# Banded attention scores: two products a block, with high and low queries in the two halves of the partitions

## What is computed

```
def swa_sink_attention(q, k, v, sinks):
    ...
    qc = q.reshape(b, nc, CHUNK, A_KV_HEADS, grp, d)
    kb = window_chunks(k.reshape(b, nc, CHUNK, A_KV_HEADS, d), A_WINDOW_CHUNKS)
    ...
    sc = jnp.einsum('bnqkgd,bnjkd->bnkgqj', qc, kb).astype(jnp.float32) * (d ** -0.5)
    ...
    p = e / (jnp.sum(e, -1, keepdims=True) + jnp.exp(sink - m))
    o = jnp.einsum('bnkgqj,bnjkd->bnqkgd', p.astype(v.dtype), vb)
```

## Time and profile before

| | us |
|---|---|
| median of 3 runs | 2661.86 (2660.55 to 2664.36) |
| profiled execution | 2663.14 |
| its span, first to last instruction | 2661.4 |
| its mean granted TensorE clock | 0.969 |
| PE busy | 2491.0 |
| DVE busy | 1658.8 |
| ACT busy | 1217.2 |
| POOL busy | 452.3 |
| end of the first stage's last product | 545 |

### The profile page before, as it was taken

One profiled execution on the slowest core, in us unless ns is written; L12 is line 12 of the kernel. 1 busy time (PEld: TensorE's weight loads), 2 busy tenths in 40 slices (PEclk: granted clock), 3 DMA queues, 4 the chain that ended last, 5 costly groups with the idle time before them and its releaser, 6 DMA issues. The chain is left out here.

```text
span 2661.4 us, 42306 instructions
## 1 busy us (share of the span) xinstructions
PE 2491.0 (94%) x12879; PEld 2092.6 (79%) x12880; DVE 1658.8 (62%) x3322; ACT 1217.2 (46%) x2075; POOL 452.3 (17%) x526
## 2 busy tenths in 40 slices
PE   5999999979999999998999999499999999999990
PEld 4888888868888888887788887388888888888880
DVE  5655455567677776766644455775785557657856
ACT  4333232244454544545111112375785557657856
POOL 0111111110110111100223331111211121112110
PEclk9999999989999999999999999599999999999995
DMA  6333333566756757535544434487897789769957
GB/s 199 122 106 102 102 102 102 153 182 194 213 182 194 216 172 205 196 132 214 177 136 139 142 111 166 171 293 278 284 382 245 226 296 327 242 225 324 381 158 260
DMA packets 233100, 535.86 MB, mean 201 GB/s; under 512 B 42945, under 2 KB 93377, under 8 KB 230961
## 3 DMA queue, kind: packets, MB, share of 16 engines
q1 hardware_dynamic: 164560, 422.55, 45.9%
q0 software_dynamic: 16416, 56.57, 8.8%
q10 hardware_dynamic: 52032, 55.61, 6.0%
HBM read 415.63 MB, written 119.01 MB: 201 GB/s over the span
## 5 line engine op out<-in xcount | busy, mean ns | idle before, releaser
L2543 DVE TENSOR_TENSOR e_wl<-rw_raw,e_wh 128x1024 fp32r<-128x1024 f32 (+1 forms) x384 | 446.6, 1218 | 24.7 <-ACT e_wh L2456 24.6
L2456 ACT ACTIVATE e_wh<-rw_raw 128x1024 fp32r<-128x1024 f32 (+1 forms) x384 | 376.9, 1049 | 6.5 <-PEq L74 6.5
L1228 PE MATMUL b_pg<-b_g_wh,jb_w_low 128*128 128x512 f32 x1024 | 336.6, 402 | 1.4 <-DVE b_g_out L1437 1.1
L2406 PE MATMUL e_p_gu<-e_wh,e_xh 128*128 128x512 f32 (+1 forms) x784 | 310.8, 396 | 0.8 <-DVE e_xl L2548 0.8
L2408 PE MATMUL e_p_gu<-e_wl,e_xh 128*128 128x512 f32 (+1 forms) x784 | 306.4, 391 | 0.0
L2407 PE MATMUL e_p_gu<-e_wh,e_xl 128*128 128x512 f32 (+1 forms) x784 | 305.9, 390 | 0.0
L1228 PEld LDWEIGHTS b_pg<-b_g_wh,jb_w_low 128*128 128x128 f32 x1024 | 185.1, 189 | 36.1 <-issue 3.8
L1286 ACT ACTIVATE b_th<-b_t 128x512 fp32r<-128x512 f32 (+3 forms) x160 | 85.3, 533 | 263.4 <-PE b_t L1210 255.2
L1228 PE MATMUL b_pg<-b_g_wl,jb_w_low 128*128 128x512 f32 x512 | 204.5, 400 | 0.0
L1377 DVE TENSOR_SCALAR_CACHE_REDUCE b_sc<-b_s 128x512 f32<-128x512 f32 (+4 forms) x320 | 175.8, 580 | 34.8 <-PE b_s L1199 32.7
L386 PE MATMUL j_pg<-qkv_w_hi,j_xh 128*128 128x512 f32 (+1 forms) x512 | 192.4, 376 | 2.4 <-DVE qkv_w_lo L682 2.4
(11 more groups left out here) (414 smaller groups left out, 5529.3 us busy)
## 6 DMA issues: line engine op xcount, KB each, us to landing
rw_raw<-w_gate_up SPq DMA_DIRECT2D x256, 512.0 KB, 6.3
rw_raw<-w_down SPq DMA_DIRECT2D x128, 512.0 KB
jb_w_low<-xt_hi SPq DMA_DIRECT2D x64, 512.0 KB, 3.8
jb_w_low<-xt_lo SPq DMA_DIRECT2D x64, 512.0 KB, 4.8
gates<-b_g_out ACTq DMA_DIRECT2D x64, 256.0 KB, 5.8
m_gt<-gates SPq DMA_DIRECT2D x16, 1024.0 KB, 8.3
jb_lead<-qk_hi SPq DMA_DIRECT2D x36, 256.0 KB, 7.1
jb_lead<-qk_lo SPq DMA_DIRECT2D x36, 256.0 KB, 7.8
```

Source lines behind the costliest of these rows:

```text
L1228: last = nc.tensor.matmul(pg[:], x_side, w_side, start=(q == 0), stop=(q == PASSES - 1))
L2406: nc.tensor.matmul(p_gu[p][:], xh[:, at], hi, start=(k == 0), stop=False)
L2456: nc.scalar.activation(wh[:, slot(e, s), :], raw[:, s:s + 1, :], ACT.Copy).then_inc(w_hi, 1)
L2543: nc.vector.tensor_tensor(wl[:, slot(e, s), :], raw[:, s:s + 1, :], f(wh[:, slot(e, s), :]), ALU.subtract).then_inc(w_lo, 1)
```

## The change

A group's queries get a tile of their own over all 128 partitions: `qa[:, g]` has the high queries of g in the 64 rows of g and their low queries in the other 64. `ks[:, g]` has the high keys of g in both halves. The low keys of both groups stand in a new tile `kl`, each in its own rows. One product of `qa[:, g]` with `ks[:, g]` over 128 rows then gives high by high plus low by high, and a second one over the 64 rows of g gives high by low. A block is made of two products in place of three, a unit of 8 in place of 12.

To fill these places, ACT's high copy is made for each group apart (64 partitions each), DVE's low part too, DVE copies the high keys to the other half, and ACT keeps the old low keys with an instruction of its own. To make room for `kl`, `by_sin` moves into the tile `lg`, where the lambdas were loaded; these are loaded later, after the last rotation, behind the store of the last tile's pieces.

```
@@ __init__ of Chunk0, project_phase
-        by_sin = ph.sb("by_sin", [P, BANK])
+        by_sin = chunk0.by_sin
...
-        qa = ph.sb("qa", [P, 2, A_Q], F32R)
-        ks = ph.sb("ks", [P, 2, 3 * CHUNK], F32R)
+        qa = ph.sb("qa", [P, A_KV, A_Q], F32R)
+        ks = ph.sb("ks", [P, A_KV, 3 * CHUNK], F32R)
+        kl = ph.sb("kl", [P, 3 * CHUNK], F32R)
...
+        def rows_of(g):
+            return slice(g * HD, (g + 1) * HD)
+
+        def banded_of(r, g, rows):
+            if r == 0:
+                return qa[rows, g, :].rearrange("p (c i n) -> p c i n", c=2, n=CHUNK)
+            return ks[rows, g, 0:P]
@@ load_chunk0 and the end of SP's work
-                for n, lam in enumerate(lambdas):
-                    sp.dma_start(chunk0.lam[:, n, :], lam.to_broadcast([P, HD])).then_inc(chunk0.lam_in, 16)
...
             store_rows(sp, STAGED0[2], STAGED0[3], slice(SEQ - P, SEQ), last_stored)
+            sp.wait_ge(rotated, 4 * NT + 2)
+            for n, lam in enumerate(lambdas):
+                sp.dma_start(chunk0.lam[:, n, :], lam.to_broadcast([P, HD])).then_inc(chunk0.lam_in, 16)
             sp.wait_ge(v_lo_done, 2 * (NT - 1) + 4)
@@ scores_of
+                def seen(keys, b):
+                    return keys[:, 0:P] if b >= 2 else keys.rearrange("p (n c) -> p n c", c=CHUNK)[:, 0:3:2, :]
...
+                        k_hi, k_lo = seen(ks[:, g, :], b), seen(kl[rows, :], b)
...
-                    nc.tensor.matmul(out, qh[:, bs], k_hi, start=True, stop=False)
-                    nc.tensor.matmul(out, qh[:, bs], k_lo, start=False, stop=False)
-                    last = nc.tensor.matmul(out, ql[:, bs], k_hi, start=False, stop=True)
+                    nc.tensor.matmul(out, qa[:, g, bs], k_hi, start=True, stop=False)
+                    last = nc.tensor.matmul(out, qa[rows, g, bs], k_lo, start=False, stop=True)
@@ pieces, on ACT
-                            nc.scalar.activation(ks[:, :, P:P + CHUNK], f(ks[:, :, CHUNK:P]), ACT.Copy).then_inc(k_kept, 1)
+                            nc.scalar.activation(ks[:, :, P:P + CHUNK], f(ks[:, :, CHUNK:P]), ACT.Copy)
+                            nc.scalar.activation(kl[:, P:P + CHUNK], f(kl[:, CHUNK:P]), ACT.Copy).then_inc(k_kept, 1)
...
+                    if r < 2:
+                        for g in range(A_KV):
+                            own_rows = rows_of(g)
+                            done = nc.scalar.activation(banded_of(r, g, own_rows), turned_of(r, last)[own_rows], ACT.Copy)
+                        done.then_inc(qk_hi_done, 1)
@@ low, on DVE
+                    if r < 2:
+                        for g in range(A_KV):
+                            own_rows, others = rows_of(g), rows_of(1 - g)
+                            if r == 0:
+                                low_part = banded_of(r, g, others)
+                            else:
+                                nc.vector.tensor_copy(banded_of(r, g, others), f(banded_of(r, g, own_rows)))
+                                low_part = kl[own_rows, 0:P]
+                            done = nc.vector.tensor_tensor(low_part, turned_of(r, last)[own_rows], f(banded_of(r, g, own_rows)), ALU.subtract)
+                        done.then_inc(qk_lo_done, 1)
```

More of the change, by code:

```diff
@@ L99, with __init__ @@
 class Chunk0:
-    def __init__(self, ph, lam):
+    def __init__(self, ph, lam, by_sin):
         self.w = ph.sb("w0", [P, KD, BANK], F32R)
@@ L109, in __init__ @@
         self.raw = self.rows[:].rearrange("p u (a n) -> p (u a) n", n=BANK)
-        self.lam = lam
+        self.lam, self.by_sin = lam, by_sin
         self.qk_in, self.v_in, self.lam_in = ph.sem("qk_in"), ph.sem("v_in"), ph.sem("lam_in")
@@ L413, in scores_of @@
                     after(pe, o_added, 2 * t + g - 1)
-                rows = slice(g * HD, (g + 1) * HD)
-                qh, ql = (qa[rows, half, :] for half in range(2))
+                rows = rows_of(g)
+                def seen(keys, b):
+                    return keys[:, 0:P] if b >= 2 else keys.rearrange("p (n c) -> p n c", c=CHUNK)[:, 0:3:2, :]
                 for b in range(NB):
                     out = blocks(unit_bank(g, last_tile))[:, b, :]
[L418 to L421, removed]
+                    if isinstance(t, int) and t == 0 and b < 2:
+                        k_hi, k_lo = ks[:, g, 0:CHUNK], kl[rows, 0:CHUNK]
                         out = out[:, 0:CHUNK]
                     else:
-                        k_hi, k_lo = (ks[rows, half, :].rearrange("p (n c) -> p n c", c=CHUNK)[:, 0:3:2, :] for half in range(2))
-                        out = out.rearrange("p (n c) -> p n c", c=CHUNK)
+                        k_hi, k_lo = seen(ks[:, g, :], b), seen(kl[rows, :], b)
+                        if b < 2:
+                            out = out.rearrange("p (n c) -> p n c", c=CHUNK)
                     bs = slice(b * P, (b + 1) * P)
-                    nc.tensor.matmul(out, qh[:, bs], k_hi, start=True, stop=False)
-                    nc.tensor.matmul(out, qh[:, bs], k_lo, start=False, stop=False)
-                    last = nc.tensor.matmul(out, ql[:, bs], k_hi, start=False, stop=True)
+                    nc.tensor.matmul(out, qa[:, g, bs], k_hi, start=True, stop=False)
+                    last = nc.tensor.matmul(out, qa[rows, g, bs], k_lo, start=False, stop=True)
                 last.then_inc(scores, 1)
@@ L581, in pieces @@
                             act.wait_ge(qk_lo_done, 4 * t)
-                            nc.scalar.activation(ks[:, :, P:P + CHUNK], f(ks[:, :, CHUNK:P]), ACT.Copy).then_inc(k_kept, 1)
+                            nc.scalar.activation(ks[:, :, P:P + CHUNK], f(ks[:, :, CHUNK:P]), ACT.Copy)
+                            nc.scalar.activation(kl[:, P:P + CHUNK], f(kl[:, CHUNK:P]), ACT.Copy).then_inc(k_kept, 1)
                             act.wait_ge(k_kept, t)
-                    nc.scalar.activation(staged_of(0, r), turned_of(r, last), ACT.Copy).then_inc(qk_hi_done, 1)
+                    if r < 2:
[4 more added lines that the diff above has]
+                    else:
+                        nc.scalar.activation(staged_of(0, r), turned_of(r, last), ACT.Copy).then_inc(qk_hi_done, 1)
                 def v_part(j):
@@ L810, in low @@
                     dve.wait_ge(qk_hi_done, 4 * t + r + 1)
-                    nc.vector.tensor_tensor(staged_of(1, r), turned_of(r, last), f(staged_of(0, r)), ALU.subtract).then_inc(qk_lo_done, 1)
+                    if r < 2:
[3 more added lines that the diff above has]
+                                low_part = banded_of(r, g, others)
+                            else:
+                                nc.vector.tensor_copy(banded_of(r, g, others), f(banded_of(r, g, own_rows)))
+                                low_part = kl[own_rows, 0:P]
+                            done = nc.vector.tensor_tensor(low_part, turned_of(r, last)[own_rows], f(banded_of(r, g, own_rows)), ALU.subtract)
+                        done.then_inc(qk_lo_done, 1)
+                    else:
+                        nc.vector.tensor_tensor(staged_of(1, r), turned_of(r, last), f(staged_of(0, r)), ALU.subtract).then_inc(qk_lo_done, 1)
                 if first:
@@ L2633, in program @@
         with Phase(nc, "jb") as both:
-            chunk0 = Chunk0(both, lg[:].rearrange("p t n -> p (t n)")[:, 0:4 * HD].rearrange("p (n d) -> p n d", d=HD))
+            logits = lg[:].rearrange("p t n -> p (t n)")
+            chunk0 = Chunk0(both, logits[:, 0:4 * HD].rearrange("p (n d) -> p n d", d=HD), logits[:, 0:BANK])
             with Phase(nc, "qkv") as ph:
```

## The result

| | before | after |
|---|---|---|
| median | 2662.43 (4 runs, 2660.55 to 2664.36) | 2712.53 (4 runs, 2711.34 to 2714.29) |
| profiled execution | 2663.14 | 2712.85 |
| its span | 2661.4 | 2711.1 |
| its mean granted clock | 0.969 | 0.959 |
| end of the first stage's last product | 544.9 | 595.5 |

The ratio is 1.019, 95% interval 1.018 to 1.021: slower, as forecast, but by 50 us and not by 26. The forecast was 2688 with a range up to 2704, so the direction was right and the size about half.

A forecast was written before the change was run, and what follows sets the result against it. PE sets the pace in the first stage's loop. Switches +23.8 us, waits for low queries +2.2 and lambda loads 0 give +26.0 on 2663.1, 2689.1; the median is 1.3 lower, so 2688 us, range 2683 to 2704.

The forecast's parts named there:

- What bounds the kernel: First stage's loop: PE is busy all the time and sets the pace; a tile costs the sum of PE's steps.
- The price of a switch: Score products on PE: each change between 64-row and 128-row form costs 0.15 us; +23.8 us in sum.
- The split copies: ACT's and DVE's query and key work: nothing in the loop, 1.1 us each in tiles 0 and 15, +2.2 us.
- The lambda loads: SP's queue, four loads moved behind the last pieces' store: v store about a microsecond later, hidden, 0 us.
- The clock: PE's granted clock in the loop's score stretch: the sum left it at 1.00, adding nothing.
- rival 2: Loop's score stretch: the clock also falls, 6 falls of 1.6 us, 2688 + 10 = 2698 us; chance 25%.
- The upper bound that stands in the same paragraph: Clock falls in the score stretch: at most 1.7 us each, in 15 pairs at most 25 us.
- Rival 1: Score products: switches are free within an accumulation, loads 0.11 us apart, 12.4 us faster, 2650 us; chance 8%.

The follow-up runs named there:

- the first experiment: The changed kernel with the three 64-row products of before, keeping the new layout, split and extra copies and moved lambda loads: 2666.07 us, 1.0020 of the kernel before.
- experiment 8: Changed kernel with zero-padded low keys (128 rows), first unit's probability turn behind group 2's first step, DVE starting after g = 0's copy: 2651.52 us, 0.9961.
- Experiment 2: Changed kernel with each group's low keys padded with zeros, so the second product also goes over 128 rows, no switches: 2658.27 us, 0.9986 of before.
- experiment 3: Changed kernel with a unit's four high products first and its four low ones after, 4 switches a pair: 2662.50 us, ratio 1.0005 to the kernel before.
- experiment 6: Changed kernel with the previous tile's g = 1 score unit moved behind group 1, 16 switches in two stretches: 2690.09 us, ratio 1.0109 to before.
- experiment 7: Changed kernel with zero-padded low keys (128 rows, no switches) and each product cut into two of 64 key columns: 2690.72 us, 1.0115 of before.
- experiment 4: Changed kernel with blocks ordered high, low, low, high, 8 evenly spread switches a pair: 2677.51 us, ratio 1.0059 to the kernel before.
- experiment 5: Changed kernel with high and low forms alternating only in the g = 0 unit, g = 1 zero-padded, 8 packed switches: 2672.57 us, 1.0042 of before.

## Why the prediction was right and wrong

**What bounds the kernel: right.** PE is busy for nearly all of the loop in every kernel here, and everything behind the stage moved rigidly.

**The price of a switch: right, 0.145 us against 0.15.** Two switches at the edges of a pair were a fair sample for sixteen inside it. A pair takes 4.43 us against 4.50 forecast, since the loads are 0.255 and not 0.26 us apart. The single units: 2.39 and 2.16 against 2.43 and 2.19. The second one's loads, to be held against the earlier trace rows:

```profile
582.63 0.19 PEld L440 LDWEIGHTS j_pg<-j_ks,j_qa 128*128 128x128 f32 x1
582.89 0.18 PEld L441 LDWEIGHTS j_pg<-j_kl,j_qa 64*128 64x128 f32 x1
...
584.43 0.18 PEld L441 LDWEIGHTS j_pg<-j_kl,j_qa 64*128 64x128 f32 x1
584.68 0.42 PEld L413 LDWEIGHTS j_pt<-ident,j_by_cos 128*128 128x128 f32 x4
```

The Trainium skill, "TensorEngine Tiling (Array Packing)", Key Properties, has the same rule, that a change of the tiling mode drains TensorE; the runs agree and put 0.145 us on it, for 128-column products.

**The split copies: right in kind.** Nothing in the loop from the third pair on, as the first experiment shows. In tile 15 the copies and subtractions come one after the other, each as long as one over all rows, and PE's wait is 2.37 us, 1.3 more than in the earlier trace rows and not 1.1:

```profile
563.08 1.19 ACT L600 ACTIVATE j_qa<-j_pt 64x512 fp32r<-64x512 f32 x2 [0.16 <-PE j_pt L413]
564.31 1.39 DVE L838 TENSOR_TENSOR j_qa<-j_pt,j_qa 64x512 fp32r<-64x512 f32 x2 [0.55 <-ACT j_qa L600]
565.85 0.44 PE L413 MATMUL j_pt<-ident,j_by_cos 128*128 128x128 f32 x1 [2.37 <-DVE j_qa L838]
```

DVE's 0.55 us of waiting end only when ACT has both halves, which is what experiment 8 mends. A part of this step's price I had not seen: behind waits of 2.4 us in the last tile the clock fell once for 3.4 us in five of the kernels (the changed one and those of experiments 2, 3, 6 and 7), but behind the same wait not in those of experiments 1, 4 and 5.

**The lambda loads: right.** The loads are off the path at their new place, which answers to the earlier trace rows; the v stores follow at 592.64, and the last outputs wait for PE as before, 1.4 us behind its last product. The four loads hold the queue for 2.2 us there and not for the 4.8 that the sum carried over from their old place, which changes nothing:

```profile
588.88 0.54 SPq L347 DMA_DIRECT2D lg<-lambda_q  x1
...
592.64 0.34 SPq L349 DMA_DIRECT2D v_hi<-j_staged  x1
...
596.97 2.51 SPq L281 DMA_DIRECT2D oa<-jb_rows  x4
```

**The clock: wrong, and this is the step that failed.** The sum put the clock at nothing; in the changed kernel it took some 27 us of the stage (24.7 up to the last pair, 2.7 from it on). The forecast's own sum, with the clock left up, is a good forecast of experiment 6, where the clock does stay up in the loop (2688 against 2690.1). The changed kernel is rival 2, which I gave 25% and sized at "6 falls of 1.6". There were 15, one at each pair, of 1.45 us each, and three of them twice as long. The upper bound that stands in the same paragraph, 25 us, would have given 2688 + 25 = 2713, and 2712.5 was measured. That this fits so closely is partly luck: it counts 15 falls of at most 1.7 us, while three of the falls were twice as long and a sixteenth came in the last tile, and the switches took 22.7 us and not 23.8. What misled me was the sentence "in the loop dense products stand on both sides". They do in the changed kernel, and they are what then runs at half clock: the fall comes 3.5 us into the pair and strikes group 1. The clock stayed up where dense work interrupted the stretch (experiment 6), and mostly where it came earlier (experiment 5). The Trainium skill, "TensorE: Matmul & The Clock Gate", HAM oscillation, ties the fall to long idle gaps; I did not rest on it, and the runs differ from it, since PE is busy for 1.00 of every microsecond from 305 to 321, about the fall at 313. The fall of the earlier trace rows was the weaker evidence for that, as PE had been idle for 1.81 us shortly before it. What sets off a fall stays open: the runs show in which stretches it came, and no more.

The range was wrong by the same step. With the mechanism seen in the earlier trace rows, its trigger unknown and its bound worked out, the range had to reach at least to that bound, 2713.

**Rival 1 had a fault that did not matter here.** It put the gain of a kernel without a price at 12 us. Experiment 2 is that kernel, and it gained 3: the slack of 0.64 us at the turn of the probabilities, which I had looked at only in the direction in which it grows, is used up in the other. With the turn moved and the low part started earlier the gain was 10 us.

## What to carry to other kernels

Count the changes of form in a stream of products, not only the products. Here a stream that alternates between 128 and 64 rows pays 0.145 us for each change, more than the 0.11 us that a product takes, so filling unused rows with zeros or ordering the products by form is faster than alternating. And when an edit makes a stretch of PE thinner, let the range reach to a fall of the clock at every such stretch, priced by the dense work that follows it; placing dense products between two thin stretches can take that back without removing a single thin product.

When a stretch on the bounding engine is to become shorter, look up the slack of the next step that waits for another engine: what goes beyond it isn't gained until that step is moved.

## What was unexpected of the hardware

- The granted clock fell to 0.50 with PE busy without a gap: at 15 of 15 pairs that take 4.43 us with 16 switches, 7 of 15 and 2 of 15 with 8 switches (spread and packed, 3.28 us), at none with 4 or 0 switches (2.70 and 2.12 us), never in the loop where the 16 stand in two places, and at 5 of 15 without any switch, with 64-column products over 3.91 us. In experiment 1 it fell once, behind the first of 15 pairs of the old form (2.98 us), and in the kernel before never, with the same products. Each of these falls lasted 3.4 us or 6.8. The counts are of one execution each.
- DVE's copy of the high keys from SBUF to SBUF (64x128) takes 0.22 us, but 1.20 when it starts while POOL is adding: it ends when POOL does, at 337.0 here, and likewise at 301.1 and 371.5 in two other tiles. Its neighbour L838, which reads PSUM, takes 0.28. The rows of the changed kernel, the last of them from the last tile, where POOL adds nothing meanwhile:

```profile
334.72 2.21 POOL L531 TENSOR_TENSOR j_by_cos<-j_by_cos,lg 128x512 f32<-128x512 f32 x1 [5.60 <-DVE lg L818]
335.80 1.20 DVE L836 CAST j_ks<-j_ks 64x128 fp32r<-64x128 f32 x1
337.02 0.28 DVE L838 TENSOR_TENSOR j_kl<-j_pt,j_ks 64x128 fp32r<-64x128 f32 x1
337.31 0.22 DVE L836 CAST j_ks<-j_ks 64x128 fp32r<-64x128 f32 x1
...
567.93 0.22 DVE L836 CAST j_ks<-j_ks 64x128 fp32r<-64x128 f32 x1
```

  It cost nothing here, since PE waits in the loop for nothing that DVE makes there. In tiles 1 to 14 the first copy takes 1.20 us and ends 0.07 to 0.09 after POOL, the second 0.22 or 0.23 with no addition beside it; in tile 0 the second starts during POOL's addition, takes 0.91 and ends 0.08 after it; in tile 15 both take 0.22. No run took POOL's addition away, so that it is the cause is read from these tiles. The Trainium skill, "SBUF — State Buffer", 🔬 SBUF: two separate sides, says that DVE and GpSimd share a pair of ports as an exclusive lock, which concerns DVE instructions in a two-port mode or with two SBUF inputs; the rows agree with such a lock, and do not tell the copy's mode.
